# Modulations of two transformer blocks: from sums over K folded by TensorE to one multiply-and-sum per output column on VectorE

## The reference

```python
sc = silu(c)
for layer in range(2):
    mod = sc @ w_mod[layer] + b_mod[layer]            # (1024) @ (1024 x 6144)
    shift1, scale1, gate1, shift2, scale2, gate2 = split(mod, 6)
    h = rmsnorm(x, g_attn[layer]) * (1 + scale1) + shift1
    o = mixer_layer(h, ...)      # h @ w_in (3078 columns), three attentions, @ w_out
    x = x + gate1 * o
    h = rmsnorm(x, g_mlp[layer]) * (1 + scale2) + shift2
    u, g = split(h @ w_up[layer], 2)                  # 2 x 2816 columns
    x = x + gate2 * ((silu(conv(g)) * u) @ w_down[layer])
```

## Time and profile before

| what | value |
|---|---|
| median of 3 runs | 1901.79 us (1900.43 to 1902.78) |
| the profiled execution | 1901.98 us |
| its span in the trace | 1900.2 us |
| busy: TensorE, VectorE, ScalarE, GpSimd | 86%, 41%, 16%, 10% of the span |
| moved | 599.99 MB, mean 316 GB/s |
| first block | about 0 to 752 us of the span |

### The profile page before, as it was taken

One profiled execution on the slowest core, in us unless ns is written; L12 is line 12 of the kernel. 1 busy time (PEld: TensorE's weight loads), 2 busy tenths in 40 slices (PEclk: granted clock), 3 DMA queues, 4 the chain that ended last, 5 costly groups with the idle time before them and its releaser, 6 DMA issues.

```text
span 1900.2 us, 25296 instructions
## 1 busy us (share of the span) xinstructions
PE 1630.8 (86%) x10752; PEld 939.0 (49%) x10752; DVE 771.6 (41%) x1506; ACT 309.0 (16%) x819; POOL 191.0 (10%) x177
## 2 busy tenths in 40 slices
PE   8999999999999999999875866757999875766757
PEld 4455999444579974574432232322575432232322
DVE  1586788877737876676000000002576000000001
ACT  1142111021511110352000000001253000000000
POOL 0011034000214510320000000000220000000000
PEclk9999999999999999999996878979999997987979
DMA  9992998444365643846999999999946999999998
GB/s 361 344 350 95 330 339 283 152 136 177 106 200 194 224 157 108 275 177 268 426 432 427 428 431 424 431 430 409 314 178 259 425 433 428 428 430 424 433 429 336
DMA packets 166323, 599.99 MB, mean 316 GB/s; under 512 B 21072, under 2 KB 79952, under 8 KB 142672
## 3 DMA queue, kind: packets, MB, share of 16 engines
q1 hardware_dynamic: 165982, 598.04, 80.5%
q10 hardware_dynamic: 242, 0.53, 0.1%
HBM read 594.76 MB, written 3.80 MB: 315 GB/s over the span
## 4 chain that ended last, share of the span: by engine, by line
PE 62%; DMA 23%; another core or an unknown queue 6%; DVE 4%; ACT 2%; SPq 1%; issue 1%; POOL 0%; DVEq 0%; ACTq 0%; POOLq 0%
DMA far<-in_w_gate 13%; PE ps L1798 11%; PE ps L1433 7%; PE ps L1460 7%; DMA far<-in_w_down 7%; PE ps L1387 5%; PE ps L1058 4%; PE ps L1227 4%; PE ps L1504 4%; PE ps L1329 3%; PE ps L1676 3%; PE ps L1535 3%; PE ps L1818 2%; DMA ring<-in_w_gate 2%
## 5 line engine op out<-in xcount | busy, mean ns | idle before, releaser
L1798 PE MATMUL ps<-ring,near 128*32 128x256 f32 x2560 | 192.5, 467 | 95.6 <-DMA ring<-in_w_gate 47.9
L3565 DVE TENSOR_TENSOR near<-ps,near 128x512 f32<-128x512 f32 x16 | 10.7, 670 | 488.6 <-PE ps L1798 488.6
L1798 PEld LDWEIGHTS ps<-ring,near 128*32 128x32 f32 x2560 | 94.4, 133 | 187.3 <-DMA ring<-in_w_up 53.9
L1818 PE MATMUL ps<-far,near 128*32 128x512 f32 x448 | 94.1, 671 | 49.8 <-DMA far<-in_w_down 46.1
L1798 PE MATMUL ps<-far,near 128*32 128x256 f32 x1024 | 82.2, 491 | 49.1 <-DMA far<-in_w_gate 25.7
L1433 PE MATMUL ps<-near,ring 128*128 128x128 f32 x960 | 114.7, 275 | 0.0
L1433 PEld LDWEIGHTS ps<-near,ring 128*128 128x128 f32 x960 | 111.0, 192 | 1.0 <-issue 1.0
L1387 PE MATMUL ps<-near,ring 128*128 128x128 f32 (+1 forms) x704 | 100.2, 304 | 0.0
L1387 PEld LDWEIGHTS ps<-near,ring 128*128 128x128 f32 x704 | 94.0, 191 | 5.8 <-issue 1.0
L3581 DVE COPY near<-ps 128x512 f32<-128x512 f32 x8 | 5.5, 691 | 210.5 <-PE ps L1818 210.0
L1058 PE MATMUL ps<-ring,near 128*128 128x512 f32 x192 | 84.9, 596 | 0.9 <-ACT near L1952 0.9
(11 more groups left out here) (387 smaller groups left out, 2510.5 us busy)
## 6 DMA issues: line engine op xcount, KB each, us to landing
ring<-in_w_gate SPq DMA_DIRECT2D x22, 4096.0 KB, 48.9
ring<-in_w_up SPq DMA_DIRECT2D x14, 4096.0 KB, 52.8
far<-in_w_down SPq DMA_DIRECT2D x14, 4096.0 KB, 52.9
ring<-in_w_mod SPq DMA_DIRECT2D x24, 2048.0 KB, 12.9
ring<-in_w_up SPq DMA_DIRECT2D x44, 1024.0 KB, 9.6
far<-in_w_gate SPq DMA_DIRECT2D x8, 4096.0 KB, 49.5
ring<-in_w_down SPq DMA_DIRECT2D x8, 4096.0 KB, 52.7
near<-in_w_down SPq DMA_DIRECT2D x8, 4096.0 KB, 52.8
```

What stands on the lines that cost most here:

```text
L1798: last = mm(ps[2 * part + e // 2][j * CAP:(j + 1) * CAP, e % 2 * 2 * P:(e % 2 + 1) * 2 * P], xsT[:, k, e * CAP:(e + 1) * CAP], expert_row( ...
L1818: last = mm(ps[n][e * CAP:(e + 1) * CAP, :], hidT[:, e, k, :], expert_row(n0, e, k)[:, n * N:(n + 1) * N], start=k == 0, stop=k == KD - 1)
```

## The change

w_mod is handed over transposed, so that the outputs are rows and K (1024) runs along a row of 4 KB. A w_mod tile is now `[128 outputs, 4 groups, 1024]`. `csilb` is silu(c) broadcast to all partitions.

- `modulation(q)` on VectorE replaces `accumulate`, the fold on TensorE and `mod_out`: four instructions of 128 x 1024 (`tensor_tensor_reduce`: multiply by `csilb`, sum along the row, start from b_mod), each giving one column of 128 outputs. It frees the slot itself (`b1_mod_read`).
- Gates come out as columns (`gcol`). SP stores them to a row in DRAM (`store_gate`) and loads them back broadcast to all partitions (`load_gate`); the b_mod broadcasts go.
- The head: w_mod's shift1 and scale1 of layer 0 come in eight transfers of 1 MB, transfer k with the 128 shifts and 128 scales of chunk k of the stream (chunks 4 to 7 are waited for in pairs), and w_in tiles 0 to 2 are loaded in quarters. For each k, `head_gain(k)` makes two reductions and the gain, `head_row(k)` and ScalarE scale chunk k of the stream, TensorE multiplies tiles 0, 1 and 2 by it.
- x is loaded in two halves. ScalarE makes silu on 128 x 1024 (`csilb`) in place of 128 x 8. The stream's raw copies in `h8` are now four of 128 x 512, three of them by ScalarE.
- Layer 1: w_mod tiles 10 and 11 move from w_up's tiles 6 and 7 to behind w_out (`MOD_AFTER`). `modulation` of tile 4 stands around `joined(3, 0)`, and both gate1 tiles are done within w_in; before, tile 5 was summed after attention.

```diff
-SUM_AT = {2: (4,), 3: (5,), 4: (6, 7), 5: (8, 9)}
+MOD_READ = {2: (4,), 3: (5,), 4: (6, 7), 5: (8, 9)}
...
-FOLD_AFTER = ({...}, {("in", LAST_IN): (0, 1), ("up", 6): (2,), ("up", 7): (3,)})
+MOD_AFTER = ({...}, {("in", LAST_IN): (0, 1), ("out", 1): (2, 3)})
...
+            def head_mod(k):
+                src = a["w_mod"][0, 0:2 * D, :].rearrange("(s n p) k -> p n s k", s=2, p=P)[:, k, :, :]
+                dst = slot_at(k // 2).rearrange("p (n s k) -> p n s k", n=2, s=2)[:, k % 2, :, :]
+                sp.dma_start(dst, src).then_inc(arrived[b1_slot(k // 2)] if k % 2 else sems[HEAD_MOD[k // 2]], 16)
...
+            def slot_free(t):
+                was = t - SLOTS
+                l, kind, j = B1_TILES[was]
+                if was < FAST:
+                    sp.wait_ge(*first_block[0].at("b1_gain_ready", 2 * was + 2))
+                elif kind == "mod":
+                    L = 0 if (l, j) in MODS[0] else 1
+                    sp.wait_ge(*first_block[L].at("b1_mod_read", MODS[L].index((l, j)) + 1 - (0 if L else FAST)))
+                else:
+                    sp.wait_ge(tile_done, b1_used(was))
...
+            head_mod(0)
+            head_rows(0, 0)
+            head_mod(1)
+            head_rows(1, 0)
+            head_mod(2)
+            head_mod(3)
+            slot_free(FAST + 2)
+            head_rows(2, 0)
+            for h in range(1, KD // 2):
+                if h > 1:
+                    head_mods(h)
+                for i in range(HEAD_IN):
+                    head_rows(i, h)
...
+            def store_gate(l, g, read):
+                i = 2 * l + g
+                sp.wait_ge(*read)
+                sp.dma_start(grows[i].rearrange("(t p n) -> p t n", t=2, n=4),
+                             gcol[:, 8 * i:8 * i + 8].rearrange("p (t n) -> p t n", t=2)).then_inc(sems["gate_stored"], 16)
...
+                slot_free(t)
+                if (L, kind, j) == (0, "mod", 10):
+                    store_gate(0, 0, first_block[0].at("b1_mod_read", 2))
+                if (L, kind, j) == (0, "out", 0):
+                    load_gate(0, 0)
...
                 if L == 0:
                     pe.wait_ge(sems["first_tab_loaded"], 16)
-                    unread(5)
+                    unread(3)
                     flip_stream(0, 0)
                     flip_stream(0, 1)
-                    pe.wait_ge(sems["csil"], 1)
-                    modulation_raw(0)
...
-                    pe.wait_ge(*stream.at("b1_stream_by_act", 8))
-                    pe.wait_ge(*stream.at("b1_stream_by_dve", 8))
+                    unread(3)
+                    for h in range(KD // 2):
+                        for i, k in ((0, 2 * h), (1, 2 * h), (0, 2 * h + 1), (1, 2 * h + 1), (2, 2 * h), (2, 2 * h + 1)):
+                            pe.wait_ge(*stream.at("b1_stream_by_act", k + 1))
+                            linear1(i, IN1_ORDER[i], 0, (k,))
+                            pe.wait_ge(*stream.at("b1_stream_by_dve", k + 1))
+                            linear1(i, IN1_ORDER[i], 1, (k,))
...
-                            for q in MOD_AT[i - 1]:
-                                modulation(q)
...
+                def weighed(v, col, l, o, name):
+                    nc.vector.tensor_tensor_reduce(v, v, csilb, 1.0, cc1(l, "b_mod", o, 1), ALU.mult, ALU.add, col)\
+                        .then_inc(s.up(name), 1)
...
                     weights_sum("t4", 1)
+                    modulation(0, range(0, 1))
                     joined(3, 0)
+                    modulation(0, range(1, 3))
                     joined(4, 0)
                     rotate("A", 16, 16)
...
-                    accumulate(0, range(0, 4))
+                    modulation(0, range(3, 4))
+                    modulation(1, range(0, 1))
                     joined(7, 2)
+                    modulation(1, range(1, 2))
                     joined(5, 2)
-                    accumulate(0, range(4, KD))
+                    modulation(1, range(2, 4))
...
-                accumulate(1 if L else 10)
...
+                modulation(2 if L else 10)
+                dve.wait_ge(sems["gate_loaded"], 32 * L + 16)
                 out_residual(0, 0)
                 if L:
-                    mod_out(1)
-                    dve.wait_ge(*s.own())
+                    modulation(3, range(0, 2))
                 out_residual(0, 1)
```

More of the change, by code:

```diff
@@ L104, in _b1_tiles @@
                 tiles += [(0, "mod", q) for q in MOD_AT[i]]
-        tiles += [(MODS[l][q][0], "mod", MODS[l][q][1]) for q in FOLD_AFTER[l].get(("in", LAST_IN), ())]
+        tiles += [(MODS[l][q][0], "mod", MODS[l][q][1]) for q in MOD_AFTER[l].get(("in", LAST_IN), ())]
         tiles.append((l, "out", 0))
@@ L108, in _b1_tiles @@
             tiles.append(t)
-            tiles += [(MODS[l][q][0], "mod", MODS[l][q][1]) for q in FOLD_AFTER[l].get(t[1:], ())]
+            tiles += [(MODS[l][q][0], "mod", MODS[l][q][1]) for q in MOD_AFTER[l].get(t[1:], ())]
     return tiles
@@ L116 @@
 B1_N = len(B1_TILES)
+B1_RANK = [sum(kind != "mod" for _, kind, _ in B1_TILES[:t + 1]) for t in range(B1_N)]
+B1_DONE = B1_RANK[-1]
 B1_SHIFT = -B1_N % SLOTS
@@ L1316, in _ @@
                 pe.wait_ge(*s.at("b1_qk_ready", 8))
-                def folds(step):
-                    for q in FOLD_AFTER[L].get(step, ()):
-                        modulation(q)
                 def out1(c, n, ks=(2, 3, 4, 5, 0, 1, 6, 7)):
@@ L1394, in _ @@
                 pe.wait_ge(*s.at("b1_mix_added", 3))
-                folds(("out", 1))
                 up(0, 0, P)
-                pe.wait_ge(*s.at("b1_mod_ready", 2 if L else 11))
                 flip_stream(2 * L + 1, 1)
@@ L1985, in qk_store @@
+                    act.wait_ge(*s.own())
+                    for k in range(KD):
+                        act.wait_ge(*s.at("b1_gain_ready", k + 1))
+                        v = h8[:, k, 0:P]
+                        av(v, v, ACT.Identity, scale=acol[:, k:k + 1], bias=modc[:, k:k + 1]).then_inc(stream.up("b1_stream_by_act"), 1)
                 def qk_store(u):
@@ L2989, in _ @@
                 if L == 0:
-                    mod_out(10)
-                    accumulate(11, range(3, KD))
+                    modulation(11, range(2, 4))
                 out_residual(1, 1)
@@ L3110, in _ @@
                     up_fourth(j)
-                    up_gated(j - 1)
-                    if j in SUM_PARTS[L]:
-                        accumulate(*SUM_PARTS[L][j])
+                    product(j - 1)
+                    if L == 0 and j in MOD_PARTS:
+                        modulation(*MOD_PARTS[j])
                     if j == UPT - 1:
@@ L3677 @@
         "rpb": _np.ascontiguousarray(i["rpb_2"][:, :, 4:11, :].reshape(DEPTH * NAH * 7, 31)),
-        "g_final": i["g_final"].reshape(1, D),
+        "g_final": i["g_final"].reshape(1, D), "c": i["c"].reshape(1, D),
+        "w_mod": _np.ascontiguousarray(i["w_mod"].transpose(0, 2, 1)),
     }
-    for n in ("w_mod", "b_mod", "w_in", "w_out", "w_up", "w_down", "w_in_2", "w_out_2", "w_uq_2", "w_ukv_2",
+    for n in ("w_in", "w_out", "w_up", "w_down", "w_in_2", "w_out_2", "w_uq_2", "w_ukv_2",
               "w_router_2", "conv_w_2"):
```

421 lines of the change are left out of this document (136 added, 285 removed).

## The result

The changed kernel takes **1891.08 us** (median of 4 runs, 1887.89 to 1892.49) against 1902.13 us for the kernel before on the same chip: ratio 0.9941, 95% interval 0.9924 to 0.9958, so 11 us faster. The forecast was 1876 us, 25.5 us faster, with a range of 1865 to 1890. Direction right, size wrong, and 1 us outside the range. That lies inside the range, but still 12 us above the forecast sum, so it does not bear the sum out.

What follows compares the result with a forecast made beforehand. TensorE bounds the first block, with VectorE and transfers close behind. Head 12.4, folds 17.0, copy 1.0, layer 1's w_up 1.7, minus layer 1's wait 6.6, give 25.5 us: 1901.8 to 1876 us, range 1865 to 1890.

Steps and rivals of the forecast that it cites:

- Reduction, folds, stage behind: VectorE's reductions every 1.15 us; 20 folds leaving TensorE gain 17.0 us; the second block only shifts with the first.
- half-rate rival: VectorE's reductions, both operands in SBUF, take 2.2 us each: about 12 us slower, 1914 us; chance 0.07.
- 1.7 + 1.7: Layer 1's w_up: two folds leave TensorE, and its idle 1.7 us go.
- Head, 12.4 forecast: Up to the end of w_in tiles 0 to 2: TensorE runs from 16.9 to 58.2 us, gaining 12.4 us.
- loses 0.5 us or so to the quarters: Head: TensorE waits about 0.5 us in all for quarters of w_in tiles 1 and 2.
- The stage behind the head, 6.1 forecast: Layer 0's w_in from `gate_sums` to the flips: gain grows from 12.4 to 18.5 us through folds and the copy.
- Everything is in time, with 2 to 5 us in hand: Layer 0's w_in behind the head: transfers and VectorE deliver before TensorE asks, 2 to 5 us early.
- the 1.0: End of layer 0's w_in: the copy behind the last fold comes earlier, gaining 1.0 us beyond the fold.
- no new wait: Layer 0's w_up: w_mod tiles land 5 to 8 us before VectorE's reductions would make TensorE wait.
- the first rival: Transfers bind the shorter stage behind the head, losing 2.2 to 12 us; transfers or VectorE late: chance 0.20.
- Layer 1's wait, 6.6 forecast: Layer 1's w_in: w_mod tile 4's reduction ahead of `joined(3, 0)` delays the flips 6.6 us; bounds 5.5 to 9.
- Behind the flips and in layer 1's attention, +1.7 forecast: From layer 1's first flips to w_up: gain grows from 20.4 to 22.1 us.

Runs made afterwards that it cites:

- e3: Changed kernel with layer 0's w_mod tiles 17 and 18 loaded or read later in w_up: 1890.24 us, ratio 0.9929 to the kernel before.
- e0: The changed kernel as it is, measured again: 1888.52 us, ratio 0.9919 to the kernel before.
- e6: Changed kernel with layer 0's `modulation(4)` behind the copy of w_in tile 2, `rotate("B")` and `forget_gate`: 1885.89 us, ratio 0.9906 to the kernel before.
- e10: Changed kernel with four unread 128x512 products on TensorE in front of layer 0's `gate_fold`: 1884.99 us, ratio 0.9921 to the kernel before.
- e1: Changed kernel with layer 1's first three reductions of modulation tile 4 behind `forget_log` and `joined(3, 1)`: 1878.16 us, ratio 0.9868 to the kernel before.
- e5: Kernel before, with half of layer 1's `accumulate(0, ...)` moved in front of `joined(3, 0)`: 1909.28 us, ratio 1.0035 to the kernel before.
- e2: Changed kernel with layer 0's `modulation(4)` just behind the copy of w_in tile 2: 1888.41 us, ratio 0.9923 to the kernel before.
- e4b: e4 run once more: 1874.70 us, ratio 0.9861 to the kernel before.
- e7: Changed kernel with layer 0's w_in tile 3 issued ahead of tables, forget gate's weights and rows: 1887.32 us, ratio 0.9933 to the kernel before.
- e8: e4 with layer 1's w_mod tiles 10 and 11 loaded behind w_up tiles 3 and 5, gate stores moved: 1886.21 us, ratio 0.9921 to the kernel before.
- e4: Changed kernel with the changes of e1, e6 and e3 together: 1876.29 us, ratio 0.9861 to the kernel before.
- e9: Changed kernel with the changes of e1 and e6 together: 1877.19 us, ratio 0.9869 to the kernel before.

## Why the prediction was wrong in size

*Reduction, folds, stage behind.* Right. The half-rate rival is ruled out: 1.20 us per reduction with both operands in SBUF, where it needed 1.8 to decide anything. The Trainium skill ("Vector Engine (DVE) Microarchitecture Reference", "Points that are easy to get wrong") has halved throughput for an instruction of scalar-tensor-tensor shape with two such sources. That does not show here, at 1.17 ns per column; whether this instruction (`CUSTOM_DVE_ANT_0` in the trace) is of the shape that the page means, no run shows. The folds' time came back wherever nothing else stepped in: w_up of layer 0 in e3 took 146.3 us against 153.1 before, 6.8 less for 8 folds of 0.84; w_up of layer 1 took 142.0 against 145.7, the forecast 1.7 + 1.7. The second block moved with the first.

*Head, 12.4 forecast, 10.5 measured.* The first product started at 15.8 us, 1.1 earlier than forecast, and the end came 1.8 later. TensorE's timeline of the changed kernel:

```profile
15.81 7.54 PE L1053 MATMUL ps<-ring,near 128*128 128x512 f32 x16 [1.62 <-ACT near L1916]
24.53 3.67 PE L1053 MATMUL ps<-ring,near 128*128 128x512 f32 x8 [1.17 <-DMA ring<-in_w_in]
28.91 31.14 PE L1053 MATMUL ps<-ring,near 128*128 128x512 f32 x72 [0.71 <-DMA ring<-in_w_in]
```

From 28.91 us on there is no gap, so the last chunks of w_mod, which landed at 43.1 instead of the forecast 41.1, held nothing. The head took 44.2 us instead of 41.3, and what was lost lies in front of 28.91: TensorE waited for quarters of w_in that landed at 24.4 and 28.8. The prediction had this as "loses 0.5 us or so to the quarters", and its sum, 16.9 + 41.3, leaves even that out. The transfers were a little slower than taken: 2.56 us from one w_mod chunk's landing to the next instead of 2.45, 1.3 to 1.6 us for a quarter instead of 1.35. In the other runs with this head it ended between 58.8 (e0) and 60.4 us.

*The stage behind the head, 6.1 forecast, 1.4 measured.* The step that failed is "Everything is in time, with 2 to 5 us in hand". It had "tile 4's reductions end at 64.6", from a landing at 60. The tile landed at 64.5. In front of it w_in tile 3 landed at 59.3 instead of 55: 2.2 us of that came with the head's last quarter (47.4 instead of 45.2), the rest is in the tables and rows, which were in flight until 53.8. The sentence also checked TensorE's needs at the wrong place: it asked when `rotate` is done, and overlooked that `gate_fold` waits for the copy of tile 2, which stands behind these reductions. From `gate_sums` to the flips the changed kernel took 19.2 us, the kernel before and e6 15.3. Of these 4 us, 2.0 are idle and most of the rest is clock (e10).

Almost all of the rest of the 4.7 us is a term of the sum that was never there, the 1.0: "fold aside, 1.0 us more comes back", read from the chain, which passes over the copy at 123.63. TensorE's own timeline before and after:

```profile
122.38 1.05 PE L1012 MATMUL ps<-tab,far 128*128 128x1 f32 x8
123.29 1.07 PE L1111 MATMUL ps<-tab,near 128*128 128x128 f32 x8
```

```profile
111.41 1.09 PE L1089 MATMUL ps<-tab,near 128*128 128x128 f32 x8
```

The first row is the fold. Before, the flips started right behind it, when the copy (123.55 to 124.23) had not begun. They start 1.7 us behind the last product before and 0.8 us after, and the 0.9 us between is the fold. So this copy was not in TensorE's way.

*Layer 0's w_up, "no new wait".* Wrong, by 3.8 us in the profile: 150.1 us against the 146.3 that e3 shows to be there. The prediction looked at the landings of the w_mod tiles, not at those of w_up. With the folds gone from TensorE the transfers of tiles 13 to 18 (share 1.02 to 1.10 from 200 to 260 us) do bind, the first rival, at a place where the prediction had not looked for it: w_up tile 5 landed at 238.1, and GpSimd's sums and then TensorE waited for it. e3 shows the cause of the gap, 2 us; the other 2 us are clock. That later tiles earn something in the whole kernel is not shown.

*Layer 1's wait, 6.6 forecast.* Mechanism and place right, and sized right as a wait: 16.2 - 9.0 = 7.2 us in the profile, 7.1 in e1, 7.7 in e5 (9.4 at the flips, less 1.7 that it was late at w_down). The w_mod tile landed 7.6 us after its issue (420.5 to 428.1). The forecast 7.4 was near; the 0.6 us faster landing of its lower bound no run shows. Not counted was the clock behind it, 1.7 us (1.6 in e0). The 7.7 of e5 contain 2.6 us of low clock too. The change of order was worth 10.4 us in the medians, two fifths of the whole gain forecast, and 4 us more than the term. The wait and the clock behind it make 8.7 of it; the traces of e0 and e1 also differ by the low clock around 246 us and in attention, which comes and goes between runs.

*Behind the flips and in layer 1's attention, +1.7 forecast, -3.0 measured.* Of the 4.7 us lost, 1.7 are the clock just told. The other 3.0 are one more drop. At 480 to 488 us the clock was 0.50 to 0.65, at 425 GB/s of transfers, behind gaps of together 0.9 us at the flips. Of the 12 profiled runs of this kernel and its variants 7 had this low clock and 5 did not (e2, e4b, e7, e8, e10), with much the same gaps and, e8 aside, the same transfers. e4 and e4b are one kernel; windows of e4, then of e4b:

```profile
468.00:472.00 4.00, 4.00 (x14) 2.53 (x15) 1.49 (x9) 1.15 (x6) 0.00 (x0) 0.50 0.99 418
```

```profile
468.00:472.00 4.00, 4.00 (x33) 2.75 (x31) 3.64 (x21) 3.20 (x14) 0.00 (x0) 1.00 1.03 434
```

It cost 3.0 us here: from the flips to w_up e4 took 96.8 us and e4b 93.8. The kernel before took 95.5, so e4b has the forecast 1.7 in full. The kernel before did not show it in its two profiles (its own and e5's). Whether the change makes it more frequent is open.

The ledger of the profiled execution, lost against the forecast: head 1.9, layer 0's w_in 4.7, its attention and w_up 4.2, layer 1's w_in up to the flips 0.6, from there to w_up 4.7; w_up gave 0.3 more than forecast. That makes 15.8 of the 15.9 us between 25.5 and 9.6. In the medians, e4b has 26.7 us, so as much as the forecast was to be had by another order alone. That the two numbers agree is luck: the forecast contains a wait of 6.6 us that e4b has not, and without it, it would be 32 us. The other 5 are still missing there: 1.2 in the head, 2.5 from layer 0's flips to w_up, of which 1.0 is the copy's term, and 2.1 in w_down. The last comes with e3's placement (112.8 us from there to the flips in e4b, 110.7 in e9 and before) and eats most of what that placement gains in w_up.

## What to carry to other kernels

When work moves to an engine that executes in order, look for every small operation that stands behind it and who waits for that, not only for the last result of the stage. A read of a tile that may not have landed belongs behind the last operation that others wait for; moving three reductions by a few lines was worth 10.4 us here, nearly as much as the whole change had brought (11.1 us). The chain of a profile is not proof that an operation is in the way: look at the waiting engine's own timeline. The order matters as much on the queue that issues transfers (e8): an order that waits for a late result holds everything behind it.

## What the runs showed of the hardware

- `tensor_tensor_reduce` of 128x1024 fp32 with both operands in SBUF: 1.28 us, 1.20 to 1.21 from one to the next, 1.17 ns per column.
- A gap of 2 to 3 us on TensorE was followed by the 1.2 GHz level for some 4 us or more in the changed kernel (2.0 us at 70, 2.3 at 247), in e0 (3.0 at both places) and in e9 (2.06 at 243), not in e1 (2.1 at 246), e7 (2.3 at 249) or e10 (2.05 at 246). Filling the gap at 70 us kept the clock up (e10). The same program fell in one run and not in another in attention (e4, e4b), where the gaps are 0.9 us. The price is 1.5 to 1.7 us for 16 instructions of 128x512, and 3.0 us in attention.
- The tables, the forget gate's 24-byte pieces and the rows took SyncE 15.8 us to issue in the changed kernel (33.66 to 49.43) and 17.6 in e7. With them in flight the transfers moved 157 and 230 GB/s at 46 to 50 and 50 to 54 us (e0), against 395 at 42 to 46 us and 425 at 58 to 62; the kernel before has the same dip (66 and 242). That the small pieces make the issue long is not shown: single loads of 2 MB took 0.4 to 9.1 us to issue in the same stretch.
